# Query tiles of a sparse attention taken in another order (7, 0, 6, 1, 5, 2, 4, 3)

## The reference, cut to what matters

```python
# compressed keys: 63 blocks of 32 keys, stride 16; a block is seen once it has ended
p_cmp = masked_softmax(s_cmp, cmp_mask);  o_cmp = p_cmp @ vcmp
# their weights choose 8 of 16 blocks of 64 keys for each query and group
imp = einsum(p_cmp.sum(heads), overlap);  sel_idx = top_k(imp, 8)
o_sel = softmax over the chosen blocks' keys that are not in the future
o_w   = softmax over the last 512 keys
o = g0 * o_cmp + g1 * o_sel + g2 * o_w
```

## Time and profile before

| | us |
|---|---|
| median of 3 runs | 3648.87 (3644.67 to 3652.53) |
| span of the profiled execution | 3653.8 |
| attention of the first layer, from and to | 628 to 994.7 |
| attention of the second layer, from and to | 2406 to 2770.2 |
| busy, whole span: PE, DVE, POOL, ACT | 3362.0, 1855.4, 1398.6, 778.1 |

### The profile page before, as it was taken

The page is one execution under the profiler, slowest core; times in us unless marked ns, Lnnn a source line. Parts: engine busy times, 40 slices in busy tenths (PEclk is TensorE's granted clock), DMA queues, the critical chain, the costliest instruction groups (busy, mean ns, idle before and its releaser), DMA issues. The chain is left out here.

```text
span 3653.8 us, 39829 instructions
## 1 busy us (share of the span) xinstructions
PE 3362.0 (92%) x15575; PEld 2708.2 (74%) x15605; DVE 1855.4 (51%) x1877; ACT 778.1 (21%) x1283; POOL 1398.6 (38%) x1096
## 2 busy tenths in 40 slices
PE   4999999888798999999989999988878999999998
PEld 3787877665587888888868888756556778888887
DVE  7743435777555544333365443467765374533333
ACT  2100012555412100001110000246552121000002
POOL 3333321667532333333323333137664233333331
PEclk6999999999898999999989999999998999999999
DMA  5434431000141222111133443300005122211111
GB/s 173 140 92 127 144 87 29 1 1 1 44 158 53 79 71 70 51 48 46 41 118 93 119 132 101 81 1 1 1 1 179 40 82 81 70 52 47 52 46 58
DMA packets 349015, 256.95 MB, mean 70 GB/s; under 512 B 9500, under 2 KB 335506, under 8 KB 348563
## 3 DMA queue, kind: packets, MB, share of 16 engines
q1 hardware_dynamic: 334642, 209.75, 19.9%
q10 hardware_dynamic: 14177, 44.56, 3.3%
HBM read 223.87 MB, written 30.41 MB: 70 GB/s over the span
## 5 line engine op out<-in xcount | busy, mean ns | idle before, releaser
L735 POOL TENSOR_SCALAR whi<-wraw 128x1024 fp32r<-128x1024 f32 x238 | 267.4, 1124 | 1857.7 <-PE lin L764 1247.7
L764 PE MATMUL lin<-hH,whi 128*128 128x512 f32 x2272 | 719.4, 398 | 46.8 <-POOL wlo L737 38.7
L764 PE MATMUL lin<-hH,wlo 128*128 128x512 f32 x2272 | 705.0, 392 | 0.0
L764 PE MATMUL lin<-hL,whi 128*128 128x512 f32 x2272 | 704.6, 392 | 0.0
L737 POOL TENSOR_TENSOR wlo<-wraw,whi 128x1024 fp32r<-128x1024 f32 x238 | 636.6, 2675 | 19.9
L764 PEld LDWEIGHTS lin<-hH,whi 128*128 128x128 f32 x2272 | 424.5, 190 | 140.2 <-POOL wlo L737 42.8
L764 PEld LDWEIGHTS lin<-hL,whi 128*128 128x128 f32 x2272 | 430.3, 189 | 91.2
L764 PEld LDWEIGHTS lin<-hH,wlo 128*128 128x128 f32 x2272 | 429.4, 189 | 90.2
L1605 DVE SCALAR_TENSOR_TENSOR xT<-lin,adac,xT 128x1024 f32<-128x1024 f32 x144 | 184.8, 1284 | 542.0 <-PE lin L764 541.7
L709 POOL TENSOR_SCALAR pTH<-pTF 128x512 fp32r<-128x512 f32 (+8 forms) x296 | 219.2, 740 | 277.4 <-ACT pTF L1193 263.2
L764 PE MATMUL lin<-hidH,whi 128*128 128x512 f32 x1024 | 315.8, 390 | 0.0
(11 more groups left out here) (234 smaller groups left out, 4294.0 us busy)
## 6 DMA issues: line engine op xcount, KB each, us to landing
wraw<-in_w_ff SPq DMA_DIRECT2D x128, 512.0 KB, 4.0
wraw<-in_w_ada SPq DMA_DIRECT2D x112, 512.0 KB, 4.8
wraw<-in_w_in SPq DMA_DIRECT2D x78, 512.0 KB, 4.0
x_keep<-xT SPq DMA_DIRECT2D x2, 4096.0 KB, 15.6
mix_keep<-tmp ACTq DMA_DIRECT2D x16, 512.0 KB, 2.6
gate_keep<-ropes ACTq DMA_DIRECT2D x16, 512.0 KB, 2.8
stG<-gate_keep ACTq DMA_DIRECT2D x16, 512.0 KB, 5.1
stM<-mix_keep ACTq DMA_DIRECT2D x16, 512.0 KB, 6.6
```

What stands on the lines that cost most here:

```text
L735: pool.tensor_scalar(whi[:, s % SPL, :], wraw[:, n % RAW, :], 1.0, 1.0, ALU.mult, ALU.mult).then_inc(w_hi, 1)
L764: mm = pe.matmul(lin[c % 2][:, hf], w, m(k)[:, hf], start=first, stop=last)
```

## The change

The order of the tiles becomes a table, and what was derived from "the tile before is qt + 1" is looked up in it.

```diff
+ORDER = [7, 0, 6, 1, 5, 2, 4, 3]
+AFTER = dict(zip(ORDER, ORDER[1:]))
+BEFORE = dict(zip(ORDER[1:], ORDER))
...
-    units, sets, flush = [("c", NT - 1)], [], []
-    for qt in reversed(range(NT)):
+    units, sets, flush = [("c", ORDER[0])], [], []
+    for qt in ORDER:
...
-                if b == "s" and g == NKV - 1 and qt:
-                    units.append(("c", qt - 1))
+                if b == "s" and g == NKV - 1 and qt in AFTER:
+                    units.append(("c", AFTER[qt]))
...
-NTH = {qt: NT - 1 - qt for qt in range(NT)}
+NTH = {qt: i for i, qt in enumerate(ORDER)}
+CHOSEN = [qt for qt in ORDER if qt >= CHOICE]
+BTH = {qt: i for i, qt in enumerate(CHOSEN)}
...
-                                    act.wait_ge(s_done, [s for s in SETS if s["qt"] == x["qt"] + 2][-1]["last"] + 1)
+                                    act.wait_ge(s_done, [s for s in SETS if s["qt"] == CHOSEN[BTH[x["qt"]] - 2]][-1]["last"] + 1)
```

More of the change, by code:

```diff
@@ L139 @@
         TILE_OF[_t] = _n
+CHOICE = N_SEL * SEL_L // P
+ORDER = [7, 0, 6, 1, 5, 2, 4, 3]
+AFTER = dict(zip(ORDER, ORDER[1:]))
+BEFORE = dict(zip(ORDER[1:], ORDER))
 def attention_plan():
-    units, sets, flush = [("c", NT - 1)], [], []
-    for qt in reversed(range(NT)):
+    units, sets, flush = [("c", ORDER[0])], [], []
+    for qt in ORDER:
         for g in range(NKV):
             for b in ("w", "s"):
-                if b == "s" and g == NKV - 1 and qt:
-                    units.append(("c", qt - 1))
+                if b == "s" and g == NKV - 1 and qt in AFTER:
+                    units.append(("c", AFTER[qt]))
                 lo = max(0, qt - WIN_T) if b == "w" else 0
@@ L193, in attention_plan @@
     return units, sets, steps, flush, groups
-CHOICE = N_SEL * SEL_L // P
 V_AFTER = 3
@@ L936, in score @@
                             if masked:
-                                mm = pe.matmul(s[:, at:at + wide], selT[:, qt % 2, g, :], blocks_of[:, k0:k0 + wide],
+                                mm = pe.matmul(s[:, at:at + wide], selT[:, BTH[qt] % 2, g, :], blocks_of[:, k0:k0 + wide],
                                                start=False, stop=not mine)
@@ L947, in transpose_group @@
                         if x["kind"] == "b":
-                            pe.wait_ge(sel_made, NTH[x["qt"]] + 1)
+                            pe.wait_ge(sel_made, BTH[x["qt"]] + 1)
                             mm = pe.transpose(o[0:64, 0:P], selb[:, :, :].rearrange("p g n -> p (g n)"), ident[:, :])
@@ L1182, in _ @@
                             if x["kind"] == "b":
-                                if NTH[x["qt"]] >= 2:
-                                    act.wait_ge(s_done, [s for s in SETS if s["qt"] == x["qt"] + 2][-1]["last"] + 1)
+                                if BTH[x["qt"]] >= 2:
+                                    act.wait_ge(s_done, [s for s in SETS if s["qt"] == CHOSEN[BTH[x["qt"]] - 2]][-1]["last"] + 1)
                                 for g in range(NKV):
-                                    ins = act.activation(selT[0:NS, x["qt"] % 2, g, :], o[32 * g:32 * g + NS, 0:P], ACT.Copy)
+                                    ins = act.activation(selT[0:NS, BTH[x["qt"]] % 2, g, :], o[32 * g:32 * g + NS, 0:P], ACT.Copy)
                                 ins.then_inc(t_free[x["bank"]], 1)
@@ L1492, in cmp_probs @@
                         if NTH[qt]:
-                            dve.wait_ge(t_done, C_GROUP[qt + 1, NKV - 1]["no"] + 1)
+                            dve.wait_ge(t_done, C_GROUP[BEFORE[qt], NKV - 1]["no"] + 1)
                         dve.tensor_tensor(cgated[:, :, 0:n], c3, bc(gate, n), ALU.mult).then_inc(c_gated, 1)
@@ L1519, in select @@
                         then(ins)
-                        if NTH[qt]:
-                            dve.wait_ge(t_done, B_GROUP[qt + 1]["no"] + 1)
+                        if BTH[qt]:
+                            dve.wait_ge(t_done, B_GROUP[CHOSEN[BTH[qt] - 1]]["no"] + 1)
                         dve.tensor_scalar(selb[:, :, 0:NS], left[:, :, :], TAKEN / 10, NEG, ALU.is_lt, ALU.mult).then_inc(sel_made, 1)
```

## The result

| | before | after |
|---|---|---|
| median of 4 runs, us | 3650.7 (3644.67 to 3652.62) | 3675.7 (3671.76 to 3679.44) |
| span of the profiled execution | 3653.8 | 3671.1 |
| attention, layer 1 (first exp to first dense matmul) | 364.06 | 377.93 |
| attention, layer 2 | 361.7 | 374.1 |
| last exp to first dense matmul, layers 1 and 2 | 12.5, 12.1 | 22.3, 21.9 |

What follows compares the result with a forecast made beforehand. A step was taken to cost the larger of its score chain or the groups' and scores' work on PE or POOL. Terms -16.7 + 12.3 - 2 + 6.5 gave +0.1 us a layer: 3649 us, range 3618 to 3676.

Steps and rivals of the forecast that it cites:

- Part 1: First halves of tiles 6, 5 and 4, which lose groups beside them: together -16.7 us a layer, bounds -21 and -5.
- The rival of bare wide steps: In tiles 6, 5, 4 PE idles awaiting exps, its clock halves: +12 us a layer, 3673 in all; chance 0.24.
- Part 2: First halves of tiles 0, 1 and 2, which gain groups and become bound by POOL: together +12.3 us a layer.
- full exclusion: Rival: POOL and DVE never run side by side in small tiles; 25.0, 23.5, 21.9 us halves, 3679 in all; chance 0.07.
- exclusion scaled by tile 6: Tile 0's first half with exclusion cost scaled by tile 6's measured half: 20.1 us, where the sum had 19.2.
- Part 3: Second halves: c units, with DVE weights and mostly a block select, trade between wide and small tiles: -2 us a layer.
- go nearly in full: In wide tiles a c unit's DVE steps were the longest thing, so removing them saves nearly their whole time.
- hide 0.92 of each: In small tiles, DVE's idle time hides 0.92 us of each moved c unit, three times, -2.8 us a layer.
- Part 4: Last exp to first dense matmul, tile 3 now last: POOL +4.3, three further groups +2.2, together +6.5 us a layer.
- Small tiles absorb more: Rival: selects fall into DVE idle time, loaded halves run 1 us less: -7.7 us a layer, 3634; chance 0.25.
- The clock in the end: Rival: PE clock rises to 1.0 in tail and tile 0's half: -5 us a layer, 3639; chance 0.08.
- the halves that keep their place: First halves of tiles 7 and 3, taken to be unchanged: 0 us.

## Why the prediction was wrong, step by step

Three terms of the sum failed, all to the same side: the c units (-2 in a layer, measured +3.9), the loaded small halves (+12.3, measured +17.0) and the end (+6.5, measured +9.8).

- **Part 1, relief of the wide halves: right.** -16.9 and -18.8 against -16.7. The rival of bare wide steps is out: no such half took more than 17.5, at a clock of 0.90 or more.
- **Part 2, the loaded small halves: right in kind, 4.7 us too small.** POOL's work was priced well (17.7, 17.1, 16.3 against 17.0, 16.3, 15.4, in all 2.3 short). The rest over it was 2.5, 2.8 and 3.7 where I had added 2.2 each. I had set aside full exclusion because by my sum tile 6's half would have needed 27.1 us and took 21.8. That sum was wrong: I added the mean of a high part, 0.75, to that of a low part, 0.72, and the means of POOL's rows already hold the time in which DVE kept it waiting. In the trace before a high part is 0.62 in the median, and the shortest scalings of 1024, 640 and 128 columns are 1.12, 0.80 and 0.37. With 1.20 for a pair, as in the end, 0.6 for the c group and these scalings, my estimate for tile 6's half is 11 x 1.20 + 0.6 + 4 x 1.12 + 4 x 0.80 = 21.5, against 21.8: so that half does not speak against exclusion. The same for tile 0's is 19.8, against 20.2 and 20.8. For tiles 1 and 2 (scalings of 896, 768, 384 and 256 at 1.01, 0.91, 0.58 and 0.48) it is 18.6 and 17.4, against 19.9 and 20.0, so there something else adds to it, and what does is open. That exclusion scaled by tile 6 came to 20.1 for tile 0 is a factor that hit, not a mechanism.
- **Part 3, the c units: wrong in sign, 5.9 us in layer 1.** It is the largest miss (6.4 in layer 2), and two steps of it failed. The first is that in a wide tile these DVE steps "go nearly in full": tiles 7, 6 and 5 gave up 21.3 us of DVE and became 16.0 shorter. Tile 5 did pass on all of it; tile 7 passed on 4.2 of 7.5. PE's work explains little of that: 33.5 less 7.5 is 26.0, and PE has 26.6, so it holds back 0.7 of the missing 3.3, and in tile 6 nothing (32.5 less 8.2 is 24.3, and PE has 23.4). The second is that a small tile was to hide 0.92 of each; it hid nothing on balance: tiles 0, 1 and 2 took 25.7 us longer for 22.2 of DVE. The waits in the second halves of tile 7 and then of tile 0, before and after each:

```profile
ACT prob L1177 <- DVE negm L1543: 12.0, 6, 4.0
DVE pTL L1549 <- POOL pTH L709: 5.2, 8, 1.0
```

```profile
DVE pTL L1556 <- POOL pTH L716: 8.7, 10, 1.9
...
ACT prob L1184 <- DVE negm L1550: 4.4, 5, 2.1
```

```profile
ACT prob L1177 <- DVE negm L1543: 2.9, 3, 1.4
```

```profile
ACT prob L1184 <- DVE negm L1550: 10.0, 6, 4.7
```

In tile 7 the exps wait 7.6 us less for the maximum, but the low parts wait 3.5 more for POOL's high parts. In tile 0 the exps wait 7.1 us more: the maximum stands behind the c unit's operations, as predicted, and nothing there hides it.

- **Part 4, the end: right in kind, 3.3 us too small.** From the last exp to the last transposes it is 11.8 us (before 5.5), +6.3 where I had +4.3: the transposes of w.1 wait for a scaling of 512 columns and begin 1.65 us after that exp (before 0.23), and from the first high part to the last scaling POOL takes 8.1 us, 986.08 to 994.19, where I had 7.2. From those transposes to the dense matmul it is 10.6 (before 7.0), +3.5 for three further groups, 1.2 each where I had 0.72. The failed term is a group's price in a row of groups: low part plus high part, not the low part alone.
- **The others.** "Small tiles absorb more" is refuted: on balance nothing was absorbed. The clock in the end did rise from 0.50 to 0.76, and the work there grew with it. "POOL and DVE in full exclusion" had the mechanism of the end, and at 25.0, 23.5 and 21.9 for the three halves too large a price, since it counted the waiting twice: 20.2, 19.9 and 20.0 were measured.

The sum of the misses is 4.7 + 5.9 + 3.3 = 13.9 in layer 1; less 0.2 in part 1 and with 0.1 in the halves that keep their place it is 13.8, and the attention is 13.9 longer where I had +0.1.

What remains open: why a c unit in a small tile costs its full DVE time and more. The select (at most 0.9 us in tile 0), POOL's scaling (0.2) and the shared banks (1.1) were each removed; the high parts on ACT took 2.0 us from tile 0's second half (23.2 to 21.2) and 1.7 from tile 1's. The clock has a part that no run separates. Tile 2's second half in the changed kernel, layer 1 and layer 2, runs the same instructions:

```profile
873.03:902.10 29.07, 20.63 (x96) 14.71 (x95) 17.48 (x46) 11.90 (x29) 13.74 (x18) 0.79 0.00 1
```

```profile
2661.24:2687.29 26.05, 17.69 (x100) 12.29 (x100) 17.48 (x46) 11.90 (x29) 13.76 (x18) 0.93 0.00 1
```

At 0.79 it takes 3.0 us more than at 0.93, and PE is busy 2.9 us more. Before, it took 22.8 at 0.78 and 20.7 at 0.92. So at like clocks c unit 4 in place of 1 costs 6.3 and 5.3 us for 4.7 of DVE, and the clock alone does not explain the excess. The second halves of tiles 0 and 1 ran at 0.67 to 0.80 after.

## What to carry to other kernels

Mixing large with small stages pays only if the small ones have room on the engine that the large one's leftovers use. Here the leftovers made POOL the busiest engine of the small stages, and a chain of DVE work moved from stages that passed on only part of the relief to stages that felt all of it. The last stage of a pipeline should be the smallest, and its price is to be taken from a row of dependent groups, both of whose passes count. To test whether two engines exclude each other, take the times of passes that nothing blocked: a mean over all passes already holds the blocked time, and the sum of both engines' means counts it twice.

## What the runs showed of the hardware

POOL's high part over 128x512 takes 0.62 us alone and 1.13 in a row beside DVE operations with two inputs in SBUF. A pair of DVE low parts takes 4.12 us in place of 1.4 beside POOL's split of a 128x1024 weight tile. So a busy time in the profile can be a blocked one, and a POOL total of 21 us in a stretch of 33 did not show that POOL's scaling held it: without that scaling the stretch took 29.7.
